# Paged K turned by VectorE in 32x32 blocks, block diagonal queries, V pages on 32 partitions

## The reference

```python
k_past = cache_k[page_table].reshape(Bd, P, H, hd)        # 8 samples, 4096 tokens, 8 heads, 64
v_past = cache_v[page_table].reshape(Bd, P, H, hd)
c_past = jnp.cumsum(lf_past, axis=1)
s_past = jnp.einsum('bqhd,bkhd->bhqk', q, k_past) * FOX_SCALE
s_past = s_past + c_q - c_past.transpose(0, 2, 1)[:, :, None, :]
p = jax.nn.softmax(jnp.concatenate([s_past, s_new], axis=-1), axis=-1)
o = (jnp.einsum('bhqk,bkhd->bqhd', p[..., :P], v_past)
     + jnp.einsum('bhqk,bkhd->bqhd', p[..., P:], v_new))
```

## Time and profile before

| | us |
|---|---|
| three timed runs | 1648.5, 1648.44, 1642.02 |
| their median | 1648.44 |
| the profiled execution | 1644.44 |
| its span, first to last instruction | 1642.8 |

### The profile page before, as it was taken

How to read it: one execution, slowest core, us unless ns; L and a number is a source line. 1 busy time by engine, 2 the same in 40 slices (tenths; PEclk the granted TensorE clock), 3 DMA queues, 4 the chain that set the end, 5 groups by cost and what they waited for, 6 DMA issues and landing times.

```text
span 1642.8 us, 33880 instructions
## 1 busy us (share of the span) xinstructions
PE 1532.9 (93%) x11281; PEld 1262.4 (77%) x11281; DVE 671.9 (41%) x1498; ACT 603.4 (37%) x1287; POOL 501.7 (31%) x952
## 2 busy tenths in 40 slices
PE   5989899998979998999999999999998899999988
PEld 5878787786768776788777887678875688888876
DVE  4444353635434444634445434454354223332221
ACT  5344444444533344324443334533344354111100
POOL 4444434420072134333343333453331123111000
PEclk9999999998989999999999999999999999999999
DMA  4131212122156566776676766777664655222521
GB/s 170 31 84 32 82 44 82 31 63 66 42 168 193 160 196 221 229 221 209 200 235 216 256 205 206 227 236 223 203 205 156 215 214 178 93 94 93 161 90 58
DMA packets 146909, 249.96 MB, mean 152 GB/s; under 512 B 37513, under 2 KB 52362, under 8 KB 146226
## 3 DMA queue, kind: packets, MB, share of 16 engines
q1 hardware_dynamic: 115154, 215.78, 41.8%
q0 software_dynamic: 31584, 32.02, 6.4%
HBM read 217.47 MB, written 30.22 MB: 151 GB/s over the span
## 4 chain that ended last, share of the span: by engine, by line
PE 58%; DMA 4%; ACT 3%; DVE 3%; issue 2%; SPq 1%; POOL 0%; DVEq 0%; ACTq 0%
PE psum L288 24%; PE psum L1895 7%; PE psum L2356 6%; PE psum L1910 4%; PE psum L2348 4%; PE psum L1943 3%; PE psum L2386 3%; DMA w_raw<-in_w_tiles 2%; PE psum L2016 1%; PE psum L2026 1%; DMA v_page<-in_cache_v 1%; PE psum L2023 1%; PE psum L1926 1%; PE psum L1986 1%; PE psum L2395 1%
## 5 line engine op out<-in xcount | busy, mean ns | idle before, releaser
L288 PE MATMUL psum<-h_hi,w_hi 128*128 128x384 f32 (+1 forms) x1344 | 495.3, 368 | 17.9 <-issue 12.9
L288 PE MATMUL psum<-h_hi,w_lo 128*128 128x384 f32 (+1 forms) x1344 | 447.2, 333 | 0.0
L288 PE MATMUL psum<-h_lo,w_hi 128*128 128x384 f32 (+1 forms) x1344 | 446.0, 332 | 0.0
L1465 POOL DMA_DIRECT2D sc<-tmp_bias x512 | 252.6, 502 | 309.0 <-PE psum L1926 306.0
L288 PEld LDWEIGHTS psum<-h_hi,w_hi 128*128 128x128 f32 x1344 | 258.1, 192 | 96.2 <-issue 91.2
L288 PEld LDWEIGHTS psum<-h_lo,w_hi 128*128 128x128 f32 x1344 | 259.3, 193 | 2.4
L288 PEld LDWEIGHTS psum<-h_hi,w_lo 128*128 128x128 f32 x1344 | 257.5, 192 | 0.0
L674 POOL DMA_DIRECT2D lfp<-in_cache_logf x256 | 124.1, 485 | 176.1 <-issue 176.1
L1895 PE MATMUL psum<-con,k_page 128*128 128x128 f32 x1024 | 152.5, 276 | 9.6 <-DVE k_t L1395 6.4
L1514 ACT ACTIVATE k_t<-psum 128x512 f32<-128x512 f32 x128 | 76.1, 595 | 186.9 <-PE psum L1895 186.9
L1895 PEld LDWEIGHTS psum<-con,k_page 128*128 128x128 f32 x1024 | 120.9, 141 | 30.3 <-issue 26.2
(11 more groups left out here) (262 smaller groups left out, 2176.1 us busy)
## 6 DMA issues: line engine op xcount, KB each, us to landing
k_page<-in_cache_k SPq DMA_DIRECT2D x256, 256.0 KB, 3.7
v_page<-in_cache_v SPq DMA_DIRECT2D x256, 256.0 KB, 3.1
w_raw<-in_w_tiles SPq DMA_DIRECT2D x63, 512.0 KB, 4.9
g_pair<-tmp_gates SPq DMA_DIRECT2D x16, 544.0 KB, 4.6
sc<-tmp_bias POOLq DMA_DIRECT2D x512, 16.0 KB, 2.9
tmp_ogla<-gate POOLq DMA_DIRECT2D x4, 1088.0 KB, 5.2
g_pair<-tmp_ogla SPq DMA_DIRECT2D x8, 544.0 KB, 8.0
x_in<-in_x_prompt SPq DMA_DIRECT2D x8, 512.0 KB, 6.1
```

What stands on the lines that cost most here:

```text
L288: m = pe.matmul(out, wt[:, s, k, :], h[:, k, t0:t0 + w], start=(k == 0 and a == 0), stop=(k == KT_ - 1 and a == 2))
L1465: pool.dma_start(sc[r0:r0 + TS, j % SLOTS, :], src.to_broadcast([TS, 512])).then_inc(sc_in[j % SLOTS], 16)
```

## The change

K pages are no longer turned by TensorE. They lie in one tile `k_page` of ten slots, and VectorE turns two pages at a time in place, in blocks of 32x32: of each page, the 32 tokens of a quarter and 32 channels change places, so that a quarter's tokens lie along the free axis on 32 partitions, one for each of 32 channels. The four quarters of a page lie on the four groups of 32 partitions. The queries of a sample are put into `q_row` (new step `ql`: 16 small matmuls with slices of the identity into PSUM and four copies by ScalarE), block diagonal: on partition group tb only columns 8 tb to 8 tb + 7 hold the queries. One product of 128 partitions then scores 32 tokens of all four quarters at once, each quarter into its own 8 rows. A head's 64 channels are two blocks, so two products accumulate.

Score rows are now (head pair, quarter, query), the two heads of a pair lie in two banks (4 and 5), and so the reductions, the exponentials and the sums come once for each of the two. The extremes and the sums are joined over the four quarters by two shuffles instead of one. The bias is stored and loaded in the order of quarters: 32 stores instead of 8, and as many loads as before (512) in two pieces of 256 values a row.

V pages land on 32 partitions each, four pages below each other, each partition holding four blocks of 32 tokens apart; two sets of four pages are kept. SP loads four K pages when a score set is done, and four V pages when a V set is done. All probability copies are ScalarE's, and they have one bank. Some small tiles share memory with others (`att`, `u_t`, `mixed`).

```diff
-LIFTED = ("kt", "pt", "pn", "od")
+LIFTED = ("ql", "pt", "pn", "od")
...
-                out += [(("kt", s, 4 * m + j), 0.45) for j in range(4)]
+                out += [(("kt", s, 2 * m + j), 0.6) for j in range(2)]
...
-    decode = [(step, cost * (0.75 if k < first else 1.5 if k > last else 1.0)) for k, (step, cost) in enumerate(decode)]
+    decode = [(step, cost * (0.8 if k < first else 1.3 if k > last else 1.0)) for k, (step, cost) in enumerate(decode)]
...
-                        src = scratch["bias"][s * H + h:s * H + h + 1, half * HALF + c * 512:half * HALF + (c + 1) * 512]
-                        pool.dma_start(sc[r0:r0 + TS, j % SLOTS, :], src.to_broadcast([TS, 512])).then_inc(sc_in[j % SLOTS], 16)
+                        src = scratch["bias"][s * H + 2 * hp:s * H + 2 * hp + 2, t0:t0 + 256]
+                        dst = sc[r0:r0 + TS, j % SLOTS, :].rearrange("p (e t) -> p e t", e=2)
+                        pool.dma_start(dst, src.unsqueeze(0).to_broadcast([TS, 2, 256])).then_inc(sc_in[j % SLOTS], 16)
```

On SP:

```diff
-            def kstep(s, p):
-                a = s * NPG + p + NK
-                if a < NB * NPG:
-                    wait_lifted(sp, "kt", s, p)
-                    load_k(a)
+            def load_v(a):
+                if a < NB * NPG:
+                    part, g = slice(a % 4 * 32, a % 4 * 32 + 32), a // 4 % 2
+                    sp.dma_start(v_page[part, g], page("cache_v", a).rearrange("o (b i) c -> (o i) b c", b=4)).then_inc(v_in_page[g], 16)
+
+            def sstep(s, n):
+                a = 4 * (s * SETS + n) + NK
+                W(sp, "sc_mm", s, n + 1)
+                for j in range(4):
+                    load_k(a + j)
```

On VectorE:

```diff
-            def kstep(s, p):
-                if copies_it("dve", "kt", s, p):
-                    lift_k(dve, dve.tensor_copy, lift_dve, s, p)
+            def kstep(s, j):
+                a = (s * SETS * 4) // 2 + j
+                slot = a % (NK // 2)
+                dve.wait_ge(k_in_page[slot], 32 * (a // (NK // 2) + 1))
+                both = k_page[:, 2 * slot:2 * slot + 2, :].rearrange("p g c -> p (g c)")
+                inc(dve.transpose(both, both), "kt_set")
```

On TensorE:

```diff
-                for hp in range(NHP):
-                    m = MM(bank[5][32 * hp:32 * hp + 32, :], q_bd[:, hp, 16 * (1 - half):16 * (1 - half) + 32], k_t[:, n % 2, hp, :],
-                           start=(half == 0), stop=(half == 1))
+                for pair in range(2):
+                    slot = (4 * (s * SETS + n) + 2 * pair) % NK
+                    col = n % 2 * P + pair * HD
+                    for e in range(2):
+                        for f in range(2):
+                            for hp in range(NHP):
+                                b = 4 * hp + 2 * e + f
+                                m = MM(bank[4 + e][32 * hp:32 * hp + 32, col:col + HD].rearrange("p (g t) -> p g t", g=2), q_row[:, b, :],
+                                       k_page[:, slot:slot + 2, 32 * b:32 * b + 32], start=(f == 0), stop=(f == 1))
...
-                    for hp in range(NHP):
-                        m = MM(bank[6][32 * hp:32 * hp + 32, 0:P], p_t[:, g % 2, col + 32 * hp:col + 32 * hp + 32],
-                               v_page[a % NV][:, hp * P:(hp + 1) * P], start=(x == 0), stop=(x == NPG - 1))
+                pe.wait_ge(v_in_page[g % 2], 64 * ((s * SETS + g) // 2 + 1))
+                stream.pass_waits(pe)
+                for tb in range(4):
+                    for e in range(2):
+                        for hp in range(NHP):
+                            col = e * P + 32 * hp + TS * tb
+                            h = 2 * hp + e
+                            m = MM(bank[6][32 * hp:32 * hp + 32, e * HD:(e + 1) * HD], p_t[:, g % 2, col:col + 32], v_page[:, g % 2, tb, h * HD:(h + 1) * HD],
+                                   start=(g == 0 and tb == 0 and e == 0), stop=(g == SETS - 1 and tb == 3 and e == 1), skip_group_check=True)
```

More of the change, by code:

```diff
@@ L58 @@
 CONST_W["later"] = (_w, 128)
+CONST_W["scan_last"] = (CONST_W["scan"][0] + 384 - LASTP, CHUNKS[2][1])
 VEC_W = {}
@@ L87, in constants @@
     put("scan", np.tile(scan, (P, 1)))
-    put("scan_last", np.tile(np.concatenate([scan[:LASTP], s % TS != 0]), (P, 1)))
+    put("scan_tail", np.tile(s % TS != 0, (P, 1)))
     put("bdones", (r[:, None] // HD == r[None, :] // HD).astype(np.float32))
@@ L602, in new_bias @@
                 def new_bias():
[L603 to L607, removed]
+                    for hp in range(NHP):
+                        src = scratch["cum_s"][2 * hp:2 * hp + 2, :].unsqueeze(0).to_broadcast([32, 2, NSAMP])
+                        sp.dma_start(newb[32 * hp:32 * hp + 32], src).then_inc(fin_in, 16)
                 def bias_rows(i):
@@ L1283, in build_gla @@
         q_sp = sb(ctx, "q_sp", [P, 3, NHB, 32])
[L1284 to L1290, removed]
+        mixed = sb(ctx, "mixed", [P, NHB * DK])
+        k_row = mixed[0:NSAMP].rearrange("p (r c) -> p r c", r=NHB)
+        vn_raw = mixed[NSAMP:NSAMP + TS]
+        wa_all = mixed[96:96 + RANK].rearrange("p (g c) -> p g c", g=GH)
+        pages = mixed[112:113, 0:NB * NPG].bitcast(I32)
+        k_page = sb(ctx, "k_page", [P, NK, FW])
+        v_page = sb(ctx, "v_page", [P, 2, 4, FW])
+        q_bd = sb(ctx, "q_bd", [P, NHP, 40])
+        q_row = sb(ctx, "q_row", [P, FW // 32, 32])
         kn = sb(ctx, "kn", [P, NHP, TS])
         sc = sb(ctx, "sc", [P, SLOTS, 512])
[L1293 to L1305, removed]
+        sc_new = sb(ctx, "sc_new", [P, 2, 2, TS + SP])
+        p_t = sb(ctx, "p_t", [P, 2, 2 * P + 24])
+        pn_t = sb(ctx, "pn_t", [NSAMP + TS, 2, NHP, TS])[NSAMP:NSAMP + TS]
+        u_t = cc("bdones")
+        smst = sb(ctx, "smst", [P, 24])
+        parts = sb(ctx, "parts", [P, 2, SP + 1])
+        SETS = NPG // 4
         per = {}
@@ L1896, in kstep @@
                 m.then_inc(lifted, 1)
             def sstep(s, n):
[L1900 to L1904 removed]
+                W(pe, "kt_set", s, 2 * n + 2)
                 if n == 0:
[L1906 removed]
+                    wait_copied(pe, "ql", s)
                     W(pe, "n_add", s, 0)
+                if n % 2 == 0:
+                    W(pe, "s_add", s, n)
```

275 lines of the change are left out of this document (133 added, 142 removed).

## The result

The changed kernel takes 1596.61 us (median of 4, 1591.11 to 1608.02) against 1648.47 in the same job: ratio 0.9696, 95% interval 0.9667 to 0.9725. It is faster by 52 us; the forecast was 97. The time lies in the range given, above the likeliest case's own (1535 to 1572), at the top of "V at half rate". The profiled execution took 1591.11 us (span 1589.5), 44 us over the sum's 1547. Those 44 us are what has to be found.

A forecast was written before the change was run, and what follows sets the result against it. TensorE was taken to bound the decode stage, busy 827 of 865 us. Sum: 1644.4 - 119 + 5 + 7 + 15 + 1 - 6 - 1 + 1 = 1547, given as 1551 us on the runs' median; range 1522 to 1612.

The forecast's parts named there:

- likeliest case: Whole kernel: the forecast of 1551 us itself, with its own range of 1535 to 1572; chance 0.52.
- V at half rate: V page loads to 32 partitions at half rate, TensorE waits for pages: 1596 us, 1575 midway; chance 0.20.
- the sum's 1547: Whole kernel: the profiled execution's 1644.4 us with all terms added; 1551 on the footing of the runs' median.
- K transposes leave, -119: TensorE, decode stage: 256 pages of 4 transposes go, -110 us, and their waits for copies, 9 us.
- +12 for the records and additions: TensorE: +5 us for denser score and V sets, +5 for ql, +2 for doubled records of new and pn.
- 64 records a set, +5: TensorE score and V sets: 64 short records cost their columns, plus 0.04 us a set over 128 sets.
- rival of a fixed price a record: TensorE score and V sets: 26 ns or more a record, 1652 to 1676 us; 0.05 slower, 0.05 near 1640 to 1656.
- A turn at 1.23 us: VectorE: each of 128 page pair transposes takes 1.23 us, 157 us in all; the scan's rate would make 2.6 us.
- Collisions on VectorE, +15 (0 to +40): VectorE's in-order queue: long turns delay masks, states, o_n and bank readings for which TensorE waits.
- kt_set costs 0, K pages are in time: Score matmuls' new wait for turned pages: K pages are issued almost a period ahead, landing in 3.7 us; 0 us.
- V pages at the rate of now; V waits -6: DMA of V pages: loads to 32 partitions keep 100 ns a packet; two sets ahead, TensorE's 5.7 us of waits go.
- ql, +5: TensorE: the new query step's small matmuls, 8 times 32 records of 32 columns, 0.6 us each time.

The follow-up runs named there:

- g2: g1 with a ring of 8 K pages and each score matmul over four pages, 32 records a set instead of 64: 1625.18 us, ratio 0.9840.
- e1: Changed kernel with each V page on every fourth partition instead of 32 neighbours, past tokens' output wrong: 1581.15 us, ratio 0.9597.
- e3: e1 with VectorE turning only 32 of the 1024 columns of each K page pair, past tokens' output wrong: 1564.14 us, ratio 0.9450.
- g1: Changed kernel with both turns of a set later, behind the scores and the V set of the set before: 1629.72 us, ratio 0.9855.
- i1: h2 with the first turn of each set moved earlier, behind the probabilities' transposition of the period before: 1574.87 us, ratio 0.9560.
- h1: e1 with 8 K slots, VectorE turning a still tile and TensorE scoring against a constant, so no K page is late: 1578.14 us, ratio 0.9569.
- e4: Kernel before with V pages landing on 32 neighbouring partitions each, V matmuls reading a constant: 1667.75 us, ratio 1.0100.
- h2: Changed kernel with a set's four V pages asked for in partition order 0, 64, 32, 96: 1593.30 us, ratio 0.9645.

## Why the prediction was right, and where it was short

The main gain came by the mechanism that was forecast, the transposes leaving TensorE. But the case given 0.52 did not come, and that the time lies so close to the 1596 of "V at half rate" is luck: of that rival's 45 us its mechanism brought 15, and the rest came from terms that stood nowhere in the sum, or stays open.

- *K transposes leave, -119.* Right in kind and size: no such row is left, and TensorE's busy time in the stage fell by 89 us in spite of the lower clock. With +12 for the records and additions, 98 were forecast, and 89 + 15 for the clock is 104 (96 to 111 for the digits of the clock).
- *64 records a set, +5.* Right: 1.03 us a set where 0.99 + 0.04 was said. The rival of a fixed price a record, and with it the 25 ns of the Trainium skill, "TensorE: Matmul & The Clock Gate", section "Wait — 56ns, not 53.3ns?", is out for such runs in four column groups: (1.10 - 0.22)/63 = 14 ns apart, with 0.22 the median of one record. Halving their number (g2) changed a set by 0.02 us.
- *A turn at 1.23 us.* Right to the digit (1232 ns); VectorE does not hold the chain by its rate.
- *Collisions on VectorE, +15 (0 to +40).* Sized about right: 17 us between e1 and e3 (24 by the ratios). Their place was wrong: the prediction measured them by the wait for o_n, which rose from 12.0 to 15.5 us, but without turns (e3) it is as long as with them (e1); what the turns add is many small waits. Their order weighs as much as their sum: moving them a part of a period later cost 33 us (g1), and moving one earlier was one of two edits that together gained 22 (i1).
- *kt_set costs 0, K pages are in time.* The cost is right, the reason wrong: VectorE does wait 27.5 us for K pages, and h1 shows no cost of it.
- *V pages at the rate of now; V waits -6.* This is the step that failed most: "I take the first end, as two sets are in flight and 22% of the engines' time is free." Packets take 122 ns and not 100; the V wait did not go but became 10.8 us. e1 and e4 price it at 15 and 17 us. The rival had the slow packets right and a price of 24 to 45, since it doubled the packets of the V pages. An estimate: the 22 ns over all packets, put on V's alone (128 x 256 = 32768 of 77473), are 52 ns each, half as much again and not twice. By that a period needs 9.1 + 1.7 = 10.8 us of DMA work, less than TensorE's 812/64 = 12.7; on the stage's average the DMA engines did not set the pace, single pages were late. The rival's price also rested on the period of 11.6 us: with the sum's own 768 us a period is 12.0, and even twice the packets, 12.3 us, would have cost 64 x 0.3 = 19 us.
- *ql, +5.* A term was missing. I priced its matmuls and not the wait of the scores for ScalarE's copies, which the order puts behind the exponentials: 7.7 us, read from the trace and not tried.
- *The clock.* No term stood for it. The granted clock in the stage fell from 0.99 to 0.97, which on 738 us is the 15 us named above. The loss comes from stretches at the half level, 1.2 GHz. One of them, behind a pause, in i1 in stretches of 4 us (columns as in the earlier trace rows), around the 4.6 us that TensorE waits for o_n:

```profile
626.00:630.00 4.00, 3.02 (x17) 1.99 (x15) 0.00 (x0) 3.83 (x17) 3.71 (x7) 1.00 0.95 229
630.00:634.00 4.00, 0.35 (x3) 0.38 (x3) 2.61 (x4) 2.47 (x7) 0.40 (x1) 0.79 0.75 165
634.00:638.00 4.00, 4.00 (x72) 3.42 (x70) 1.15 (x3) 1.54 (x3) 1.26 (x3) 0.50 0.34 118
638.00:642.00 4.00, 4.00 (x25) 3.28 (x21) 1.74 (x5) 0.39 (x1) 0.00 (x0) 0.86 0.44 104
642.00:646.00 4.00, 4.00 (x82) 3.16 (x82) 3.05 (x6) 1.79 (x7) 0.54 (x1) 1.00 0.87 263
```

This pause of 4.6 us is followed by some 5 us of work at half speed, so it costs half as much again. The clock goes with idle time in the main, not strictly: 0.95 in g1, with 800 - 707 = 93 us idle, 0.98 in e3, with 58, but 0.96 in h2, with 66, under the changed kernel's 0.97 with 71.

Together: V pages 15, the q_row wait 8 and collisions 2 over their term (9 by the ratios) make 25 of the 44 us; part of the 15 us of clock lies inside these, as the clock rose where the V waits went (e1). What stays open is the rest of the idle time that even e3 shows, where neither V nor the turns are in the way: it takes 1564 where the forecast without its collisions would be 1536, and the q_row wait (8.8 there) is in these 28. TensorE waits there for o_n (17.2 us in the fixed stretch; 12.0 in the whole stage before) and for the mask (9.5). A likely reading is that the K transposes had filled TensorE while the chain of attention, state and norm ran through VectorE and ScalarE, and that this filling is gone; no run tests it. The change also altered the costs by which the two lists are merged (0.8 and 1.3 for 0.75 and 1.5), and so the order of that chain against the projections, and it gave ScalarE all copies of the probabilities; neither was tried apart either.

## What to carry to other kernels

Give a transfer's partitions as much thought as its bytes: 32 neighbours made the queue's mean packet 18% (e4) to 25% (e1) slower, 32 at a stride of four did not. Price each new producer's place in its in-order queue (here copies behind ten exponentials), not its duration alone. A long wait in a profile is not yet a cost: VectorE's for K pages and ScalarE's for weights could be taken away or cut by two thirds without a gain, so try that before mending them.

## What the runs showed of the hardware that I had not expected

- 256 KB to 32 neighbouring partitions: 117 to 122 ns a packet on the queue's mean; to 32 partitions at a stride of four: 97; landings 4.9 and 3.6 us.
- A queued transfer's neighbours matter a little: with partitions 0, 64, 32, 96 in turn 116 ns a packet and 4.4 us to landing.
- 64 short matmuls in four column groups start 14 ns apart, far under what one matmul alone takes (0.22 us).
- VectorE turns 128x1024 f32 in 32x32 blocks in place in 1.23 us, which is what its copies (689 ns for 512 columns, 420 for 256) come to when drawn out to 1024.
